# Gate, up and up projections of the last three feed-forwards: seven products of 128-token quarters in place of eight multiplications per output tile

## The reference

```python
def swiglu(u, w_gate, w_up, w_down):                     # first model, D_FF = 2816
    return (jax.nn.silu(u @ w_gate) * (u @ w_up)) @ w_down
...
    m = rmsnorm(h, norm_mlp_pre[i])                      # second model, D_FF_2 = 4096
    m = jnp.square(jax.nn.relu(jnp.einsum('bsd,df->bsf', m, w_up[i])))
    m = jnp.einsum('bsf,fd->bsd', m, w_down[i])
    h = h + rmsnorm(m, norm_mlp_post[i])
```

## Time and profile before

| | |
|---|---|
| median of the runs | 2246.71 us |
| span of the profiled execution | 2246.0 us (the page gives no other time for it) |
| TensorE busy | 2163.1 us (96%) |
| vector engine busy | 1082.7 us (48%) |
| ScalarE busy | 462.0 us (21%) |
| weights read from HBM | 286.15 MB, mean 128 GB/s over the span |

### The profile page before, as it was taken

The page is one execution under the profiler, slowest core; times in us unless marked ns, Lnnn a source line. Parts: engine busy times, 40 slices in busy tenths (PEclk is TensorE's granted clock), DMA queues, the critical chain, the costliest instruction groups (busy, mean ns, idle before and its releaser), DMA issues.

```text
span 2246.0 us, 33411 instructions
## 1 busy us (share of the span) xinstructions
PE 2163.1 (96%) x14268; PEld 1514.0 (67%) x14268; DVE 1082.7 (48%) x1944; ACT 462.0 (21%) x1004; POOL 139.0 (6%) x148
## 2 busy tenths in 40 slices
PE   6999999989999999999998999999999999999998
PEld 3447878554688885456466885686785488768646
DVE  2675555477645446652353114585324428642443
ACT  2433211352300000031253000223210022311001
POOL 0004333000000000011100000002000000200000
PEclk9999999999999999999999999999999999999999
DMA  8221444504322224445103444333344433234441
GB/s 325 75 75 40 153 153 155 177 20 187 150 75 94 93 76 150 170 144 136 57 8 131 158 154 169 141 113 113 131 150 169 155 145 119 107 131 150 169 170 74
DMA packets 41665, 289.86 MB, mean 129 GB/s; under 512 B 5040, under 2 KB 6448, under 8 KB 7216
## 3 DMA queue, kind: packets, MB, share of 16 engines
q1 hardware_dynamic: 39344, 279.99, 34.0%
q0 software_dynamic: 1312, 3.15, 1.1%
q10 hardware_dynamic: 864, 4.61, 0.5%
HBM read 286.15 MB, written 1.05 MB: 128 GB/s over the span
## 4 chain that ended last, share of the span: by engine, by line
PE 91%; DVE 5%; ACT 2%; issue 1%; DMA 1%; SPq 0%; ACTq 0%; DVEq 0%
PE banks L1009 22%; PE banks L414 15%; PE banks L1571 12%; PE banks L1470 7%; PE banks L2726 6%; PE banks L2068 6%; PE banks L1751 2%; PE banks L1775 2%; PE banks L649 1%; PE banks L789 1%; PE banks L1771 1%; PE banks L2720 1%; PE banks L452 1%; PE banks L502 1%; PE banks L804 1%
## 5 line engine op out<-in xcount | busy, mean ns | idle before, releaser
L414 PE MATMUL banks<-normed,weight_ring 128*128 128x256 f32 (+1 forms) x1280 | 294.8, 393 | 7.8 <-DVE normed L566 5.7
L414 PEld LDWEIGHTS banks<-normed,weight_ring 128*128 128x128 f32 x1280 | 245.2, 192 | 56.7 <-issue 15.3
L1009 PE MATMUL banks<-arena 128*128 128x512 f32 x392 | 186.2, 593 | 0.7 <-DVE arena L1627 0.5
L1470 PE MATMUL banks<-normed,weight_ring 128*128 128x256 f32 x704 | 153.9, 382 | 3.4 <-ACT normed L580 3.4
L1009 PE MATMUL banks<-weight_ring,arena 128*128 128x512 f32 x338 | 157.1, 593 | 0.0
L1470 PEld LDWEIGHTS banks<-normed,weight_ring 128*128 128x128 f32 x704 | 134.9, 192 | 22.4 <-ACT normed L580 3.8
L1009 PEld LDWEIGHTS banks<-arena 128*128 128x128 f32 x392 | 74.1, 190 | 93.6 <-issue 92.3
L2726 PE MATMUL banks<-normed,weight_ring 128*128 128x256 f32 x576 | 127.6, 381 | 5.8 <-DVE normed L566 2.9
L2068 PE MATMUL banks<-normed,weight_ring 128*128 128x512 f32 x288 | 126.1, 593 | 0.0
L2726 PEld LDWEIGHTS banks<-normed,weight_ring 128*128 128x128 f32 x576 | 108.6, 190 | 22.6 <-issue 5.0
L974 DVE TENSOR_TENSOR arena<-weight_ring 128x512 f32<-128x512 f32 x67 | 46.2, 690 | 144.2 <-PE banks L1009 144.2
(11 more groups left out here) (455 smaller groups left out, 3422.4 us busy)
## 6 DMA issues: line engine op xcount, KB each, us to landing
weight_ring<-in_weights SPq DMA_DIRECT2D x266, 1024.0 KB, 4.8
residual<-in_tokens ACTq DMA_DIRECT2D x1, 2048.0 KB, 12.7
mix<-in_rpb POOLq DMA_DIRECT2D x32, 64.0 KB, 3.7
constants<-in_const ACTq DMA_DIRECT2D x1, 1953.5 KB, 12.6
out<-residual SPq DMA_DIRECT2D x1, 1024.0 KB, 4.8
branch<-arena POOLq DMA_DIRECT2D x1, 512.0 KB, 4.8
normed<-in_ple POOLq DMA_DIRECT2D x1, 512.0 KB, 3.7
vector_params<-in_vectors ACTq DMA_DIRECT2D x1, 223.0 KB, 5.8
```

The costliest lines, as they stand in the source:

```text
L414: mm = pe.matmul(K.psum[lo:hi, banks[m % nb], 0:T], K.block(first[m] + k)[:, lo:hi], rhs(k), start=(k == 0), stop=(k == n_k - 1))
L1009: return pe.matmul(self.bank[i], left, b, start=(p == 0), stop=(p == n - 1))
L1470: mm = pe.matmul(K.bank(i % 4, T), K.block(first[i] + k), u[:, k, 0:T], start=(k == 0), stop=(k == KT - 1))
```

## The change

A new class `QuarterPairs` makes a pair of output tiles from seven products for 256 tokens; its quarters have 128 tokens. Each product has four multiplications of 128 columns. Two pairs form a group, with outputs side by side in four banks, so that ScalarE's copy has 128x256 and the vector engine's four sums have the shapes of layer 0. In `gated_pairs` a pair is two neighbouring gate tiles or the two up tiles that belong to them, and a group is one of each: Silu goes over 128x512, then a multiplication of 128x512. In `squared_pairs` Relu and Square, both by ScalarE, go over 128x1024. The weight blocks are packed in quarters on the host. The weight sums of pair 0 are placed before the norm in the vector engine's program; the position tables move to the middle of the stage (vector part after group 2, ScalarE's after group 4). The down projection that follows starts with products 1 and 2 of two of its pairs (`ahead=2`), shares the weight sum buffers with the stage, and waits for its banks one by one.

```diff
-        out.append((in_quarters, interleaved)[i](pack_tiles(x["w_ffn_gate"][i], columns(FF)), pack_tiles(x["w_ffn_up"][i], columns(FF)), KT))
+        out.append(in_quarters(pack_tiles(x["w_ffn_gate"][i], columns(FF)), pack_tiles(x["w_ffn_up"][i], columns(FF)), KT))
...
-        out.append(pack_tiles(x["w_up_2"][i], columns(FF2)))
+        out.append(quarters(pack_tiles(x["w_up_2"][i], columns(FF2)), KT).reshape(-1, P, P))
...
-            self.pairs(pe, 0, self.n - 2, {3: banks_free})
+            self.pairs(pe, 0, self.n - 2, banks_free if isinstance(banks_free, dict) else {3: banks_free})
...
-def feed_forward(K, u, T, n_f, hidden, tmp, deps, k_ready, parts):
...
+class QuarterPairs:
+    H = KT // 2
...
+    def outs(self, g):
+        first = 4 * ((self.n_groups - 1 - g) % 2)
+        b = [self.K.bank(first + i).rearrange("p (i n) -> p i n", i=2) for i in range(4)]
+        return {1: b[0][:, 0], 2: b[1][:, 0], 6: b[1][:, 1], 7: b[2][:, 0], 5: b[2][:, 1], 3: b[3][:, 0], 4: b[3][:, 1], "2,6": b[1], "3,4": b[3]}
...
+    def add_weights(self, dve, p):
+        K = self.K
+        c = self.begin // CB + p
+        dve.wait_ge(K.chunk_arrived[c % RING].sem, 16 * (c // RING + 1))
+        if p >= 2:
+            need(dve, [self.hit("f_products", p - 1)])
+        step = K.in_turn(dve, "vector")
+        a11, a21, a12, a22 = (self.quarter(p, i) for i in range(4))
+        s1, s2, s3, s4 = self.s[p % 2]
+        dve.tensor_tensor(out=s3, in0=a11, in1=a21, op=ALU.subtract)
+        step(dve.tensor_tensor(out=s1, in0=a21, in1=a22, op=ALU.add))
+        step(dve.tensor_tensor(out=s2, in0=s1, in1=a11, op=ALU.subtract))
+        dve.tensor_tensor(out=s4, in0=a12, in1=s2, op=ALU.subtract).then_inc(self.sg["f_weights"].sem, 1)
...
+    def product(self, pe, p, i, k_ready=None):
+        K, H = self.K, self.H
+        g, x = divmod(p, 2)
+        left = {1: 0, 2: 2, 4: 3}.get(i)
+        if p < 2 and i in (5, 6, 7, 4):
+            need(pe, [self.hit("f_tokens", {7: 1, 5: 2, 6: 3, 4: 4}[i])])
+        if left is None:
+            need(pe, [self.hit("f_weights", p + 1)])
+            a = self.s[p % 2][{5: 0, 6: 1, 7: 2, 3: 3}[i]]
+        else:
+            K.arrived(pe, self.begin + CB * p)
+            a = self.quarter(p, left)
+        right, o = self.right(i), self.outs(g)[i][:, x * P:x * P + P]
+        for k in range(H):
+            if k_ready:
+                need(pe, k_ready(k if i == 1 else H + k))
+            mm = pe.matmul(o, a[:, k * P:k * P + P], right[:, k], start=(k == 0), stop=(k == H - 1))
+        return mm
+
+    def products(self, pe, k_ready):
+        self.product(pe, 0, 1, k_ready)
+        self.product(pe, 1, 1)
+        self.product(pe, 0, 2, k_ready)
+        self.product(pe, 1, 2)
+        self.product(pe, 0, 3)
+        for i in (7, 5, 6):
+            self.product(pe, 0, i)
+        self.product(pe, 0, 4).then_inc(self.sg["f_products"].sem, 1)
+        self.product(pe, 1, 3)
+        for i in (7, 5, 6):
+            self.product(pe, 1, i)
+        self.product(pe, 1, 4).then_inc(self.sg["f_products"].sem, 1)
+        for p in range(2, self.n):
+            if p % 2 == 0 and p >= 4:
+                need(pe, [self.hit("f_quarters", p // 2 - 1)])
+            for i in (1, 2, 4, 7, 5, 6):
+                self.product(pe, p, i)
+            self.product(pe, p, 3).then_inc(self.sg["f_products"].sem, 1)
...
+def gated_pairs(K, made, hidden, token_sums, y, k_ready, meanwhile):
...
+        made.add_tokens(dve, k_ready)
+        made.add_weights(dve, 1)
+        for g in range(n):
+            for p in (2 * g + 2, 2 * g + 3):
+                if p < made.n:
+                    made.add_weights(dve, p)
+            made.combine(dve, g)
+            need(dve, [made.hit("f_gate", g + 1)])
+            dve.tensor_tensor(out=tiles(g), in0=tiles(g), in1=part(1), op=ALU.mult).then_inc(made.sg["f_hidden"].sem, 1)
+            if g == 2:
+                meanwhile["vector"](dve)
...
+                pairs = QuarterPairs(K, u, FF // P, token_sums, pair_sums, pair_quarters, K.inverse[:, 1, 0:S])
+                K.add(vector=lambda dve, pairs=pairs: pairs.add_weights(dve, 0))
...
-            r = matmul_stage(K, FF2 // P, KT, lambda k: u2[:, k, :], S, lambda e, m, ps: e.activation(hidden[:, m, :], ps, ACT.Relu), [], k_ready=kr)
...
+            pairs = QuarterPairs(K, u2, FF2 // P // 2, token_sums, pair_sums, pair_quarters, K.inverse[:, 1, 0:S])
+            K.add(vector=lambda dve, pairs=pairs: pairs.add_weights(dve, 0))
```

More of the change, by code:

```diff
@@ L1450, in run @@
         return (lambda k: [hit("shifted", k + 1)]), *b.done()
-def feed_forward(K, u, T, n_f, hidden, tmp, deps, k_ready, parts):
[L1455 to L1471, removed]
-    def scalar(act):
[L1474 to L1482, removed]
-    def vector(dve):
[L1485 to L1489, removed]
@@ new lines, in gated_pairs @@
+def gated_pairs(K, made, hidden, token_sums, y, k_ready, meanwhile):
+    n = FF // P // 2
+    groups = [(lo, min(lo + 4, n)) for lo in range(0, n, 4)]
+    down = TokenProjection(K, hidden, FF // P, by_group(token_sums, groups), made.s, y, lambda k: [made.hit("f_hidden", k // 2 + 1)], groups, ahead=2, sets_free=made.sets_free())
+    tiles = lambda g: hidden[:, 2 * g:2 * g + 2, :].rearrange("p f n -> p (f n)").rearrange("p (q n) -> p q n", q=4)
+    part = lambda x: made.z[:, 0:4, x * P:x * P + P]
+    def scalar(act):
+        for g in range(n):
+            made.take_first(act, g)
+            need(act, [made.hit("f_quarters", g + 1)])
+            act.activation(tiles(g), part(0), ACT.Silu).then_inc(made.sg["f_gate"].sem, 1)
+            if g == 4:
+                meanwhile["scalar"](act)
+    def vector(dve):
+        made.add_tokens(dve, k_ready)
+        made.add_weights(dve, 1)
+        for g in range(n):
+            for p in (2 * g + 2, 2 * g + 3):
[6 more added lines that the diff above has]
+                meanwhile["vector"](dve)
+            if g in (4, 8):
+                down.add_tokens(dve, g // 4 - 1)
+            if g == n - 2:
@@ L1490, in vector, with squared_pairs, scalar @@
                 down.add_weights(dve, 0)
-            if f % 8 == 7 or f == n_f - 1:
-                down.add_tokens(dve, f // 8)
         down.add_weights(dve, 1)
-    K.add(tensor=tensor, scalar=scalar, vector=vector)
-    return down, [(mixed, h + n_f)]
+        down.add_tokens(dve, 2)
+    K.add(tensor=lambda pe: made.products(pe, k_ready), scalar=scalar, vector=vector)
+    return down, made.banks_free()
+def squared_pairs(K, made, hidden, token_sums, y, k_ready):
+    n = FF2 // P // 4
+    groups = [(4 * g, 4 * g + 4) for g in range(4)]
+    down = TokenProjection(K, hidden, FF2 // P, by_group(token_sums, groups), made.s, y, lambda k: [made.hit("f_hidden", k // 4 + 1)], groups, ahead=2, sets_free=made.sets_free())
+    tiles = lambda g: hidden[:, 4 * g:4 * g + 4, :].rearrange("p f n -> p (f n)")
+    by_quarter = lambda g: tiles(g).rearrange("p (x q n) -> p q x n", x=2, q=4)
+    def scalar(act):
+        for g in range(n):
+            made.take_first(act, g)
+            need(act, [made.hit("f_quarters", g + 1)])
+            act.activation(by_quarter(g), made.z[:, 0:4].rearrange("p q (x n) -> p q x n", x=2), ACT.Relu).then_inc(made.sg["f_gate"].sem, 1)
+            need(act, [made.hit("f_gate", g + 1)])
+            act.activation(tiles(g), tiles(g), ACT.Square).then_inc(made.sg["f_hidden"].sem, 1)
+    def vector(dve):
+        made.add_tokens(dve, k_ready)
+        made.add_weights(dve, 1)
+        for g in range(n):
+            for p in (2 * g + 2, 2 * g + 3):
+                if p < made.n:
+                    made.add_weights(dve, p)
+            made.combine(dve, g)
+            if g in (2, 4, 6):
+                down.add_tokens(dve, g // 2 - 1)
+            if g == n - 2:
+                down.add_weights(dve, 0)
+        down.add_weights(dve, 1)
+        down.add_tokens(dve, 3)
+    K.add(tensor=lambda pe: made.products(pe, k_ready), scalar=scalar, vector=vector)
+    return down, made.banks_free()
@@ L3114, in program @@
         token_y = R.y[:, 0:4 * 512].rearrange("p (q n) -> p q n", q=4)
+        pair_quarters = R.extra.rearrange("p (i n) -> p i n", i=6)
         for layer in range(2):
@@ L3141, in program @@
             else:
[L3142 to L3145, removed]
+                down, r = gated_pairs(K, pairs, hidden, down_sums, token_y, kr, tables)
                 root_table(K)
                 r, tiles = down.run(h, gain(layer, 3), r)
+        token_sums = [R.y[:, 512 * i:512 * i + 512].rearrange("p (k n) -> p k n", k=4) for i in range(4)]
         lat = h[:, :, S:T2]
```

91 lines of the change are left out of this document (62 added, 29 removed).

## The result

The changed kernel took 2224.99 us in the median of four runs (2213.83 to 2228.38) against 2248.03 us of before (2243.39 to 2250.3): a ratio of 0.9889, with a 95% interval of 0.9869 to 0.9909. Two further measurements of the same file gave 2218.85 us, 0.9872 (0.9847 to 0.9897), and 2217.07 us, 0.9861 (0.9836 to 0.9887). So it is faster by 23 to 33 us, about 28 (each difference is to the kernel before beside it, on its own chip). The median of 2224.99 us lies 11.6 us above the forecast of 2213.4 us.

What follows compares the result with a forecast made beforehand. TensorE bounds the kernel, busy 2163.1 of 2246.0 us; stages cost instruction count times spacing. Products -35.3 and starts +2.0 sum to -33.3 us: span 2212.7, median 2213.4 us, range 2206 to 2229.

Steps and rivals of the forecast that it cites:

- the forecast's own width: Whole kernel: 2208 to 2221 us, from spacing 111 to 112.2 ns, starts and ends +0 to +5, and slow starts.
- A: Three stages: products run at the worst short stretch's pace, 117.8 ns; 2232 us, chance 0.08.
- C: Three stages: vector engine late, a 1 us wait in each of 27 groups; 2240 us, chance 0.03.
- Pace of the products (-35.3 us): Three stages: 3024 instructions of 128 columns at 111.6 ns, set by stationary-block loads, 337.5 instead of 372.8 us.
- 108.8 ns taken for loads alone: Three stages: lower bound on instruction spacing, from 32 products of 16 columns in 3.48 us; would give -43.8 us.
- rival D: Three stages: more gain, 108.8 ns spacing and a reciprocal not delayed, -43.8 us; 2203 us, chance 0.02.
- Vector engine (0): Mid-stage: sums need 9.5 of 12.5 us per two-pair group, ready 5 to 6 us early; 0, bounds 0 to +3.
- Start (+2.0 us): Stage starts: pair 0's weight sums delay reciprocal and TensorE by 0.65 us, three times; bounds 0 to +2.7.
- 1.7 us per changed slow start: Stage starts: allowance in the forecast's width for a changed time at the low clock, 1.7 us each.
- End, weights, position tables (0): Stage end, weight fetches and tables moved inside the stage: no added time; end bounds 0 to +1.
- B: Three stages: products break apart at their heads, seven a pair, with no slack left; 2287 us, chance 0.05.
- rule on row groups: Three stages: load and product would follow each other, some 217 ns per instruction, 656 us; given no chance.

Runs made afterwards that it cites:

- version with 64 columns: Changed kernel, each product of the three stages multiplying only the first 64 of its 128 columns (output not the reference's): 2532.54 us, one execution.
- first GpSimd version: Changed kernel with pair 0's weight sums made by GpSimd, starting when the out projection's last product is done: 2221.7 us, ratio 0.9898.
- longer pause: Kernel before plus four unused 128x512 vector-engine sums between residual and the norm's reciprocal in the three stages: 2265.49 us, ratio 1.0069.
- late GpSimd: Changed kernel with pair 0's weight sums made by GpSimd, starting only after the vector engine scaled the out projection's last tokens: 2216.47 us, ratio 0.9862.
- 128 columns: Kernel before with each 256-column instruction of the three stages made as two of 128 columns, no sums: 2270.32 us, ratio 1.0089.

## Why the prediction was right, point by point

The mechanism was right, and it decided the time. The agreement of the number has luck in it. The median of 2224.99 us is outside the forecast's own width (2208 to 2221 us; its terms as written, -33.5 + 5 + 3 x 1.7, reach 2223). It is inside the stated range only because that was stretched to 2229 us for rivals A and C, and neither of them happened: what used up that room was the clock.

*Pace of the products (-35.3 us).* Right, and it was the term that decided. The load sets it: 111.6 ns with and without sums beside, and 213.5 ns at half the clock with half the columns. One reading was off without harm: the 108.8 ns taken for loads alone is an effect of the piece's edge. From the second of the 32 products of 16 columns to the last it is 1447.70 to 1451.05 us from start to start, 30 distances of 111.7 ns, the same as with 128. So there was no lower end at 108.8, and rival D had no ground. The pieces are 34.8 us shorter than before in the profiled execution (378.7 - 343.9).

*Vector engine (0).* Right: 73% busy where 9.5 of 12.5 us were worked out, no wait of TensorE in a stage. Rival C has no row for it.

*Start (+2.0 us).* Right in kind. The reciprocal came 0.55 us later, not 0.65, TensorE's pause grew by 0.63 us each. What it does to the clock was put at "1.7 us per changed slow start" in the forecast's own width, and at nothing in the sum; and for the clock elsewhere there was no term at all. Over the profiles of all unfilled kernels, the piece at the lower clock behind the pause of these stages lasted 6.8 us in 8 of 16 cases where the pause had 3.50 to 4.20 us, and 3.4 us in all 11 where it had 2.87 to 3.41. Left out are the version with 64 columns and the first GpSimd version, where low pieces stand before pauses too (from 1565.2 us, its pause comes at 1573.5). It is a count over these stages and no rule for pauses: the pause of 3.39 us before the first layer's long piece has 6.8 us behind it in the profile of before. For the changed kernel the count gives 0.5 x 1.7 x 3 = 2.6 of the 6.9 us. Where the rest stands in the changed kernel itself is not shown: its three profiled executions lost 17.7, 24.4 and 17.7 us, the worst ones (up to 35.6) have no profile, and only the second has pieces in the attention of the last layers, 3.4 us of loss. In the kernels whose profiled execution lost most (longer pause, late GpSimd, 128 columns) the attention has 20.4, 11.9 and 10.2 us.

*End, weights, position tables (0).* Right: no gap before the down projection, DMA share 0.45.

*Rivals.* A and B are out: a stretch of 130 us holds 1166 loads, 111.5 ns each, with a product's head at every eighth, so heads cost nothing though no slack is left. D is out. The Trainium skill's rule on row groups (TensorE: Matmul & The Clock Gate, Part 3, "The mechanism") would have had 656 us; the stages took 344. A danger that stood on no list is the lower clock for whole stages, as the run with 64 columns has it.

*Left open.* Why 128 columns in the last layers' stages, or a pause longer by half a microsecond, change how often the attention of these layers falls to the lower clock. Every execution has its own pattern, and a profile shows one.

## What to carry to other kernels

When products are cut into smaller ones, read the spacing of the shortest shape that the trace already has, with ever fewer columns if it can be found: where it stops falling, loads set the pace, and the saving is counted in instructions times that, not in columns. Then compare a kernel's executions by span times granted clock and by what is left, since one profile can show the plan fulfilled while the median is 10 us off. Pauses of three to four microseconds before a long stage are worth a try at filling: here it took the loss to 15.5 us where 128-column stages followed, and brought nothing sure (16.1 to 14.8 us) where 256-column ones did. When such a loss is traced to one cause, as here to the longer pause, test the kernel that has the rest of the change without it; that one lost as much.

## What the hardware showed unexpectedly

The stage with 64 columns per product ran at 1.2 GHz for 262 us on end without a gap, the same stage with 128 at 2.4 GHz but for its start. GpSimd's sums made the vector engine's scalings of 128x512 2.5 times as long (2.20 for 0.88 us), but left the residual, another operation and with PSUM as a source, at 3.23 us; which of the two makes the difference, no run here shows. Sums of 128x512 take GpSimd 1.26 us, the vector engine 0.69. At half the clock a load took 213.5 ns, 9.7 less than twice 111.6, so not all of its time follows the clock.
